# Two padding tensors that move matmul operands to 64 bytes past a multiple of 128

## The chip, the cores and the metric

The kernel runs on one core of one Trainium2 chip, as one launch. The metric is the device time in microseconds of one execution; the numbers given are medians of several runs, and one execution is taken by the hardware profiler.

## The reference, cut to what matters

Two small networks follow each other on 256 tokens of width 1024, each with two layers, all in float32. A layer of the first network is a feed-forward block, a mixer with three branches (a linear recurrence, a latent attention with 8 heads, a convolution branch) whose outputs are gated and merged, and a second feed-forward block. A layer of the second network is a mixer (16 attention heads of four kinds) and one feed-forward block with a short convolution.

```python
def swiglu(x, w1, w2):
    gu = x @ w1
    g, u = gu[..., :D_FF], gu[..., D_FF:]
    return (jax.nn.silu(g) * u) @ w2

for l in range(DEPTH):
    x = x + 0.5 * swiglu(rms_norm(x, ffn1_norm[l]), ffn1_w1[l], ffn1_w2[l])
    x = x + hybrid_mixer(rms_norm(x, mix_norm[l]), ...)
    x = x + 0.5 * swiglu(rms_norm(x, ffn2_norm[l]), ffn2_w1[l], ffn2_w2[l])
```

D_FF is 2816, so a feed-forward block holds 1024 x 5632 and 2816 x 1024 weights. All weights are read from HBM once; nothing of them is reused.

## The kernel before, in words

Activations lie transposed, features on the 128 partitions and the 256 tokens along the free dimension, in tiles of 128 features: h is 8 such tiles, the hidden layer 22. The weights are cut into blocks of 128x128, and up to 16 blocks make a unit of at most 1 MB. A unit comes by one DMA into one of two raw buffers, in a fixed order (ALL_UNITS).

To reach float32 accuracy at the rate of the faster type fp32r, a number is split into a high part (rounded to fp32r) and the low remainder. ScalarE copies raw to w_hi (split_hi, line 597), VectorE subtracts to w_lo (split_lo, line 636); there are four slots of each. Activations are split the same way: h_hi and h_lo, hid_hi and hid_lo (the hidden layer), m_hi and m_lo (the merged branches of mixer 1), o2_hi and o2_lo (the heads' outputs of mixer 2), win_hi and win_lo (windows of keys and values in mixer 2). A product of a weight block and a tile is three matmuls that add up in PSUM (product, lines 657 to 659): high with high, high weight with low activation, low weight with high activation. The weight block is the stationary operand, loaded by an LDWEIGHTS of its own for each matmul, and the activation moves, 256 columns of 4 bytes. first_products (669 to 678) and by_tiles (692 to 694) issue the same matmuls in another order. In tokens_product (710 to 712) the roles are swapped: the weights move and h or win is stationary. Other products (whole_product, 704, attention scores, transposes, norm sums) are matmuls in plain float32; the weights of these come to w_whole, w_lat, scr or sq.

A feed-forward block is an up stage of 22 units of 16 blocks (48 matmuls each on h) and a down stage of 8 output tiles with two units of 11 blocks (66 matmuls each tile on hid). Between them VectorE scales, multiplies and splits, ScalarE applies silu. In mixer 1, UNIT_ORDER1 gives the order: 11 units of two tiles on h, the recurrence, the latent projections (uq, uk), the attention, then the branch products A, B and C with their gates (24 tiles on h) and the output product on m. In mixer 2, STEPS2 gives it: nine units of features on h, the values, and 24 heads, one after the other, among which other units stand.

Every tensor of SBUF is placed by the order of its sbuf(...) line, one after the other, sizes rounded up to 32 bytes. Tensors of one `with ExitStack()` block share their place with those of the next. The first, raw, begins at byte 16,512 of each partition, which is 129 x 128. So the program before has these addresses modulo 128: raw, w_hi, w_lo, x, h_hi, h_lo, const, vec, scr, sq, acc, std and rinv at 0; rinv is 258 numbers long, so trig1, cos2, sin2 and all that begins behind them (hid_hi, hid_lo, m_hi, m_lo, feat, win, win_hi, win_lo, o2_hi, o2_lo, const2) at 32. Farther up, conv, gelu, xa and w_whole are at 0, and lat, w_lat, o1 and v2a at 64.

LAT_BLOCKS says how many of the 12 blocks of unit ("uq", 2) lie in w_lat; the others lie in sq. Line 601 copies the first, line 603 the rest.

Of the kernel before, what the change touches and what calls it, by code (L numbers as in the profile page):

```python
# [16 lines left out]
F32 = mybir.dt.float32  # L17
# [6 lines left out]
T = 256  # L24
P = 128
# [8 lines left out]
SPLIT_SLOTS = 4  # L34
AHEAD = 3
FFN_AHEAD = 4
EPS = 1e-6
MASKED = -1e30
TWO_PI = 2 * np.pi
# [250 lines left out]
def build(nc, io):  # L290
    with ExitStack() as ctx:
        def sbuf(name, shape, dt=F32, stack=ctx):
            return stack.enter_context(nc.sbuf_tensor(name, shape, dt))
# [2 lines left out]
        raw = sbuf("raw", [P, RAW_SLOTS, 16 * P])  # L296
        w_hi = sbuf("w_hi", [P, SPLIT_SLOTS, 16 * P], F32R)
        w_lo = sbuf("w_lo", [P, SPLIT_SLOTS, 16 * P], F32R)
        x = sbuf("x", [P, KT, T])
        h_hi = sbuf("h_hi", [P, KT, T], F32R)  # L300
        h_lo = sbuf("h_lo", [P, KT, T], F32R)
# [3 lines left out]
        sq = sbuf("sq", [P, 2, T])  # L305
# [3 lines left out]
        trig1 = sbuf("trig1", [P, T])  # L309
        cos2 = sbuf("cos2", [P, T])  # L310
        sin2 = sbuf("sin2", [P, T])
        ones = const[:, CONST["ones"]:CONST["ones"] + P]
        ident = const[:, CONST["ident"]:CONST["ident"] + P]
        causal = const[:, CONST["causal"]:CONST["causal"] + 384]
# [10 lines left out]
        with ExitStack() as phase:  # L325
            with ExitStack() as early:
                q1 = sbuf("q1", [P, QKV_HEADS, T], F32, early)
                k1 = sbuf("k1", [P, QKV_HEADS, T], F32, early)
            m_hi = sbuf("m_hi", [P, KT, T], F32R, phase)
            m_lo = sbuf("m_lo", [P, KT, T], F32R, phase)  # L330
            v1 = sbuf("v1", [P, 2, QKV_HEADS * VD], F32, phase)
            glu = sbuf("glu", [P, 4, T + CONV_TAPS - 1], F32, phase)
            conv = sbuf("conv", [P, 4, T], F32, phase)
            derived = sbuf("derived", [P, 64], F32, phase)
            probs1 = sbuf("probs1", [P, 2, 384], F32, phase)
            probs_t1 = sbuf("probs_t1", [P, 2, 384], F32, phase)
            row1 = sbuf("row1", [P, 16], F32, phase)
            with ExitStack() as early:
                lat = sbuf("lat", [P, 5, T], F32, early)
                w_lat = sbuf("w_lat", [P, 22 * P], F32, early)  # L340
            o1 = sbuf("o1", [P, 4, T], F32, phase)
            sbuf("rest", [P, 3, 4, T], F32, phase)
            pad_r = sbuf("pad_r", [P, 4, T + LRU_TAPS - 1], F32, phase)
            gelu = sbuf("gelu", [P, 4, T], F32, phase)
            xa = sbuf("xa", [P, 4, T], F32, phase)
            a_t = sbuf("a_t", [P, 4, T], F32, phase)
            i_g = sbuf("i_g", [P, 4, T], F32, phase)
            w_whole = sbuf("w_whole", [P, SPLIT_SLOTS * 4 * P], F32, phase)
            with ExitStack() as early:
                r_g = sbuf("r_g", [P, 4, T], F32, early)  # L350
            gate = sbuf("gate", [P, 2, T], F32, phase)
            y_b = sbuf("y_b", [P, 2, T], F32, phase)
# [205 lines left out]

        LAT_BLOCKS = 10

        def unit_kind(s):

            return UNIT_ORDER1[s % len(UNITS1) - MIX1_AT]
# [1 line left out]
        def whole_part(s, block, blocks):  # L567

            unit = unit_kind(s)
            if unit == ("uk", 0):  # L570
                return scr[:].rearrange("p k t -> p (k t)")[:, block * P:(block + blocks) * P]
            if unit == ("uq", 2) and block >= LAT_BLOCKS:
                return sq[:, 0, (block - LAT_BLOCKS) * P:(block - LAT_BLOCKS + blocks) * P]
            if unit[0] == "uq":
                at = block + (12 if unit[1] else 0)
                return w_lat[:, at * P:(at + blocks) * P]
            at = (4 * (s % SPLIT_SLOTS) if PARTED[s] else 0) + block
            return w_whole[:, at * P:(at + blocks) * P]
# [8 lines left out]
        def split_hi(act, s, more=0, half=0):  # L587
# [10 lines left out]
            if parted < n:  # L598
                count = (n - parted) // P
                cut = LAT_BLOCKS if unit_kind(s) == ("uq", 2) else count  # L600
                last = act.activation(whole_part(s, 0, cut), raw[:, s % RAW_SLOTS, parted:parted + cut * P], ACT.Copy)
# [290 lines left out]
        def ffn_act(act, l, w, at, then, split):  # L892
# [9 lines left out]
            with act.Fori(0, 4) as it:  # L902
                for u in range(4):
                    gated(u, it * 4, u % 2, lambda: split_hi(act, at + u + FFN_AHEAD, it * 4, it * 2))
            split.next = at + 16 + FFN_AHEAD
            for j in range(16, FT):
                gated(j, 0, j % 2, lambda: split.until(at + j + FFN_AHEAD))
            if l == 0 and w == 0:
                act.wait_ge(*turned(0, 1))
                act.activation(trig1[:], trig1[:], ACT.Sin).then_inc(trig_ready.sem, 1)  # L910
            if l == 0 and w == 1:
                act.wait_ge(*turned2(0, 2))
                act.activation(cos2[:], cos2[:], ACT.Sin)
                act.activation(sin2[:], sin2[:], ACT.Sin).then_inc(trig2_ready.sem, 1)
            base = at + FT + FFN_AHEAD
            l2, n2_ = then
# [21 lines left out]
        def ffn_dve(dve, l, w, at, n, then, split):  # L938
# [20 lines left out]
            for j in range(2):  # L959
                gated(j, 0, j % 2, lambda: split.until(at + j + FFN_AHEAD), j > 0)  # L960
            with dve.Fori(0, 4) as it:
                for u in range(2, 6):
                    gated(u, it * 4, u % 2, lambda: split_lo(dve, at + u + FFN_AHEAD, it * 4))
            split.next = at + 18 + FFN_AHEAD
# [1121 lines left out]
        block = ctx.enter_context(nc.Block())  # L2086
# [385 lines left out]
```

## Time and profile before

| | us |
|---|---|
| median of 3 runs | 2106.05 |
| lowest and highest run | 2103.4, 2112.19 |
| the profiled execution | 2109.53 |
| its span, first to last instruction | 2107.7 |
| PE busy in the span | 2003.4 |
| DVE busy | 1406.4 |
| ACT busy | 1160.2 |
| mean granted clock of TensorE | 0.977 |

The page gives the busy time of each engine (PE is the matmul side of TensorE, PEld its weight loads, DVE VectorE, ACT ScalarE, POOL GpSimd). Start times are measured; the ends of matmuls are modelled, so a matmul's duration (some 280 ns) is longer than the distance from its start to the next. The rows on which the prediction rests stand two sections below.

### The profile page before, as it was taken

How to read it: one execution, taken by the hardware profiler on the slowest of the kernel's cores; microseconds unless marked ns; L12 is line 12 of the kernel's file. 1: busy time of each engine (PE TensorE's matmuls, PEld its weight loads, DVE VectorE, ACT ScalarE, POOL GpSimd, SP SyncE). 2: the span in 40 equal slices, each digit the busy share in tenths (PEclk: the TensorE clock that was granted, in tenths of full speed). 3: DMA queues.
4: the chain of work that ended last, by engine and by line, in shares of the span. 5: the costliest groups of instructions: out<-in, count | busy, mean ns of one | idle time of the engine just before them, and what ended most of it. 6: DMA issues, size and time to landing. Idle time of an engine off the chain costs nothing.

```text
span 2107.7 us, 39543 instructions
## 1 busy us (share of the span) xinstructions
PE 2003.4 (95%) x15240; PEld 1901.6 (90%) x15240; DVE 1406.4 (67%) x2072; ACT 1160.2 (55%) x1847; POOL 142.3 (7%) x153
## 2 busy tenths in 40 slices
PE   7999989989999999989989999998999999898998
PEld 7999969989999999978989999976899998678997
DVE  5765887666655665788656656775588568738973
ACT  5444666554445444576455445575666457656753
POOL 1062100010000000100000001000100010002000
PEclk9999999999999999999999999998999999999999
DMA  5545433445545545443445545441245544304543
GB/s 213 206 169 185 150 125 125 151 170 184 185 156 194 198 158 186 167 151 105 153 163 181 193 149 183 162 160 41 81 164 197 173 154 152 137 3 156 202 163 116
DMA packets 53533, 329.80 MB, mean 156 GB/s; under 512 B 5936, under 2 KB 6704, under 8 KB 27952
## 3 DMA queue, kind: packets, MB, share of 16 engines
q1 hardware_dynamic: 53424, 328.34, 44.5%
q8 instruction: 69, 1.13, 0.2%
q14 instruction: 40, 0.33, 0.0%
HBM read 327.27 MB, written 1.05 MB: 156 GB/s over the span
## 4 chain that ended last, share of the span: by engine, by line
PE 61%; DVE 13%; issue 8%; ACT 6%; DVEq 5%; DMA 4%; POOLq 3%; POOL 1%; ACTq 0%; SPq 0%
PE bank L657 16%; PE bank L658 16%; PE bank L659 16%; DVE w_lo L636 5%; DMA raw<-in_w 4%; PE bank L704 3%; ACT w_hi L597 2%; DVE conv L1362 1%; PE bank L669 1%; PE bank L1651 1%; PE bank L671 1%; PE bank L1635 1%; DVEq L1356 1%; PE bank L1652 1%; PE bank L1653 1%
## 5 line engine op out<-in xcount | busy, mean ns | idle before, releaser
L636 DVE TENSOR_TENSOR w_lo<-raw,w_hi 128x2048 fp32r<-128x2048 f32 (+3 forms) x348 | 673.6, 1939 | 343.5 <-ACT w_hi L597 316.2
L657 PE MATMUL bank<-h_hi,w_hi 128*128 128x256 f32 x2704 | 779.2, 288 | 8.4 <-DVE conv L2024 3.4
L658 PE MATMUL bank<-h_lo,w_hi 128*128 128x256 f32 x2704 | 768.0, 284 | 0.0
L659 PE MATMUL bank<-h_hi,w_lo 128*128 128x256 f32 x2704 | 767.6, 284 | 0.0
L597 ACT ACTIVATE w_hi<-raw 128x2048 fp32r<-128x2048 f32 (+2 forms) x346 | 560.3, 1623 | 142.2 <-DMA raw<-in_w 118.6
L657 PEld LDWEIGHTS bank<-h_hi,w_hi 128*128 128x128 f32 x2704 | 522.0, 193 | 14.9 <-issue 8.5
L658 PEld LDWEIGHTS bank<-h_lo,w_hi 128*128 128x128 f32 x2704 | 522.1, 193 | 1.2
L659 PEld LDWEIGHTS bank<-h_hi,w_lo 128*128 128x128 f32 x2704 | 521.8, 193 | 0.0
L657 PE MATMUL bank<-hid_hi,w_hi 128*128 128x256 f32 x1056 | 295.4, 280 | 0.0
L658 PE MATMUL bank<-hid_lo,w_hi 128*128 128x256 f32 x1056 | 295.4, 280 | 0.0
L659 PE MATMUL bank<-hid_hi,w_lo 128*128 128x256 f32 x1056 | 295.3, 280 | 0.0
L657 PEld LDWEIGHTS bank<-hid_hi,w_hi 128*128 128x128 f32 x1056 | 198.5, 188 | 0.0
L658 PEld LDWEIGHTS bank<-hid_lo,w_hi 128*128 128x128 f32 x1056 | 198.5, 188 | 0.0
L659 PEld LDWEIGHTS bank<-hid_hi,w_lo 128*128 128x128 f32 x1056 | 198.5, 188 | 0.0
L897 ACT ACTIVATE scaled<-scaled 128x256 f32<-128x256 f32 x88 | 36.8, 418 | 258.3 <-DVE scaled L944 258.3
L796 POOL TENSOR_TENSOR acc<-sq 128x256 f32<-128x256 f32 x13 | 12.2, 940 | 1577.9 <-ACT sq L789 1577.7
L1362 DVE SCALAR_TENSOR_TENSOR conv<-glu,vec,conv 128x256 f32<-128x256 f32 x240 | 106.0, 481 | 10.7 <-issue 0.9
L789 ACT ACTIVATE sq<-x 128x256 f32<-128x256 f32 (+1 forms) x88 | 35.9, 410 | 123.1 <-DVE x L974 92.6
L944 DVE TENSOR_TENSOR scaled<-bank,rinv 128x512 f32<-128x512 f32 x88 | 60.6, 689 | 50.6 <-PE bank L659 37.1
L669 PE MATMUL bank<-h_hi,w_hi 128*128 128x256 f32 x224 | 64.8, 321 | 18.2 <-DVEq L1913 6.6
L800 POOL TENSOR_TENSOR acc<-acc,sq 128x256 f32<-128x256 f32 x65 | 60.3, 928 | 227.2 <-ACT sq L789 224.4
L669 PEld LDWEIGHTS bank<-h_hi,w_hi 128*128 128x128 f32 x224 | 50.8, 227 | 20.6 <-DVEq L1913 7.4
(339 smaller groups left out, 2960.5 us busy)
## 6 DMA issues: line engine op xcount, KB each, us to landing
raw<-in_w SPq DMA_DIRECT2D x198, 1024.0 KB, 4.8
raw<-in_w SPq DMA_DIRECT2D x96, 704.0 KB, 4.1
raw<-in_w SPq DMA_DIRECT2D x52, 768.0 KB, 4.2
raw<-in_w SPq DMA_DIRECT2D x8, 512.0 KB, 3.5
raw<-in_w SPq DMA_DIRECT2D x4, 576.0 KB, 3.7
x<-in_x SPq DMA_DIRECT2D x1, 1024.0 KB, 5.0
out<-x SPq DMA_DIRECT2D x4, 256.0 KB, 2.4
const<-in_const SPq DMA_DIRECT2D x1, 548.0 KB, 5.7
```

The lines of the kernel that those rows point to most:

```text
L597: last = act.activation(w_hi[:, s % SPLIT_SLOTS, 0:parted], raw[:, s % RAW_SLOTS, 0:parted], ACT.Copy)
L636: dve.tensor_tensor(w_lo[:, s % SPLIT_SLOTS, 0:n], raw[:, s % RAW_SLOTS, 0:n], w_hi[:, s % SPLIT_SLOTS, 0:n].bitcast(F32), ALU.subtract).t ...
L657: pe.matmul(out, hi, x_hi, start=start, stop=False, skip_group_check=skip)
L658: pe.matmul(out, hi, x_lo, start=False, stop=False, skip_group_check=skip)
L659: return pe.matmul(out, lo, x_hi, start=False, stop=stop, skip_group_check=skip)
L669: pe.matmul(out, w_hi[:, s % SPLIT_SLOTS, at], h_hi[:, k], start=k == 0 and half == 0, stop=False, skip_group_check=half == 1)
L704: return pe.matmul(out, whole_part(s, block, 1), y, start=start, stop=stop)
L789: act.activation(sq[:, parity], src, ACT.Square).then_inc(nm.sq_ready.sem, 1)
L800: pool.tensor_tensor(acc[:], acc[:], sq[:, t % 2], ALU.add).then_inc(nm.sq_summed.sem, 2 if t == KT - 2 else 1)
L897: act.activation(scaled[:, parity, 0:T], scaled[:, parity, 0:T], ACT.Silu).then_inc(silu_ready.sem, 1)
L944: dve.tensor_tensor(halves(scaled[:, parity]), halves(bank[:, :]), by_r(2), ALU.mult).then_inc(work.freed["v"].sem, 1)
L1362: last = dve.scalar_tensor_tensor(conv[:, t], glu[:, t, j:j + T], w, conv[:, t], ALU.mult, ALU.add)
```

## The change

Two tensors are added that nothing reads or writes, offset_h of 16 numbers (64 bytes) behind w_lo, and offset_hid of 24 numbers (96 bytes) behind sin2. They take room, so w_lat shrinks by one block: LAT_BLOCKS goes from 10 to 9 and moves to the head of the file, and the tensor `rest` (which only keeps room for lat and w_lat behind o1) is written by its new size. The third block of unit ("uq", 2) that now lies in sq runs into sq's second half, so sq is addressed flat.

The addresses modulo 128 that follow: raw, w_hi and w_lo stay at 0; x, h_hi, h_lo, const, vec, scr, sq, acc, std and rinv go from 0 to 64; trig1, cos2 and sin2 from 32 to 96; hid, m, feat, win, o2 and const2 from 32 to 64; conv, gelu, xa and w_whole from 0 to 32; lat, w_lat, o1 and v2a from 64 to 96.

```diff
@@ -34,6 +34,7 @@
 FFN_AHEAD = 4
+LAT_BLOCKS = 9
 EPS = 1e-6
@@ -296,6 +297,7 @@
         w_lo = sbuf("w_lo", [P, SPLIT_SLOTS, 16 * P], F32R)
+        sbuf("offset_h", [P, 16])
         x = sbuf("x", [P, KT, T])
@@ -309,6 +311,7 @@
         sin2 = sbuf("sin2", [P, T])
+        sbuf("offset_hid", [P, 24])
         ones = const[:, CONST["ones"]:CONST["ones"] + P]
@@ -337,9 +340,9 @@
                 lat = sbuf("lat", [P, 5, T], F32, early)
-                w_lat = sbuf("w_lat", [P, 22 * P], F32, early)
+                w_lat = sbuf("w_lat", [P, (12 + LAT_BLOCKS) * P], F32, early)
             o1 = sbuf("o1", [P, 4, T], F32, phase)
-            sbuf("rest", [P, 3, 4, T], F32, phase)
+            sbuf("rest", [P, T + (12 + LAT_BLOCKS) * P], F32, phase)
@@ -558,8 +561,6 @@
-        LAT_BLOCKS = 10
-
@@ -570,7 +571,7 @@
             if unit == ("uq", 2) and block >= LAT_BLOCKS:
-                return sq[:, 0, (block - LAT_BLOCKS) * P:(block - LAT_BLOCKS + blocks) * P]
+                return sq[:].rearrange("p a t -> p (a t)")[:, (block - LAT_BLOCKS) * P:(block - LAT_BLOCKS + blocks) * P]
```

## Rows read from the trace of the kernel before

**Rows 1.** The page, part 1: busy us, share of the span, instructions.

```profile
PE 2003.4 (95%) x15240; PEld 1901.6 (90%) x15240; DVE 1406.4 (67%) x2072; ACT 1160.2 (55%) x1847; POOL 142.3 (7%) x153
```

**Rows 2.** Windows by stage: busy us (count) per engine, PEclk, DMA, GB/s.

```profile
663.00:790.00 127.00, 127.00 (x1058) 126.89 (x1057) 80.70 (x86) 58.94 (x70) 0.00 (x0) 1.00 0.51 178
790.00:852.00 62.00, 62.00 (x530) 62.00 (x530) 33.60 (x33) 27.50 (x31) 5.90 (x6) 1.00 0.56 192
852.00:1116.00 264.00, 243.30 (x1700) 226.63 (x1699) 194.41 (x346) 158.25 (x270) 12.82 (x14) 0.98 0.42 147
1508.00:1641.00 133.00, 130.04 (x1058) 128.33 (x1058) 115.19 (x173) 89.36 (x132) 11.83 (x14) 0.99 0.48 168
...
1703.00:1902.00 199.00, 181.67 (x1166) 150.50 (x1165) 132.38 (x249) 123.94 (x275) 5.38 (x6) 0.95 0.31 107
```

**Rows 3.** Timeline, PE, up stage: start us, duration us, line, operation.

```profile
60.03 0.28 PE L658 MATMUL bank<-h_lo,w_hi 128*128 128x256 f32 x1
...
61.11 0.28 PE L658 MATMUL bank<-h_lo,w_hi 128*128 128x256 f32 x1
```

**Rows 4.** Timeline, PE in a down stage.

```profile
151.00 0.28 PE L659 MATMUL bank<-hid_hi,w_lo 128*128 128x256 f32 x1
151.12 0.28 PE L657 MATMUL bank<-hid_hi,w_hi 128*128 128x256 f32 x1
151.23 0.28 PE L658 MATMUL bank<-hid_lo,w_hi 128*128 128x256 f32 x1
...
151.94 0.28 PE L658 MATMUL bank<-hid_lo,w_hi 128*128 128x256 f32 x1
```

**Rows 5.** Timeline, PE in mixer 1 (m) and mixer 2 (weights moving).

```profile
464.13 0.28 PE L658 MATMUL bank<-m_lo,w_hi 128*128 128x256 f32 x1
...
465.19 0.28 PE L658 MATMUL bank<-m_lo,w_hi 128*128 128x256 f32 x1
...
1352.81 0.39 PE L711 MATMUL bank<-w_hi,h_lo 128*128 128x512 f32 x1
1353.04 0.40 PE L712 MATMUL bank<-w_lo,h_hi 128*128 128x512 f32 x1
```

**Rows 6.** Groups by form: count, busy us, mean ns of one, idle before.

```profile
L658 PEld LDWEIGHTS bank<-h_lo,w_hi 128*128 128x128 f32 x2704 | 522.1, 193 | 1.2
...
L658 PE MATMUL bank<-hid_lo,w_hi 128*128 128x256 f32 x1056 | 295.4, 280 | 0.0
...
L658 PEld LDWEIGHTS bank<-hid_lo,w_hi 128*128 128x128 f32 x1056 | 198.5, 188 | 0.0
...
L704 PE MATMUL bank<-o,w_whole 128*128 128x256 f32 x128 | 30.3, 379 | 0.0
...
L704 PE MATMUL bank<-conv,w_whole 128*128 128x256 f32 x128 | 29.6, 379 | 0.0
...
L711 PE MATMUL bank<-w_hi,win_lo 128*128 128x256 f32 x64 | 17.9, 280 | 0.0
```

**Rows 7.** Groups by form, DVE and ACT.

```profile
L636 DVE TENSOR_TENSOR w_lo<-raw,w_hi 128x2048 fp32r<-128x2048 f32 x198 | 452.4, 2289 | 177.7 <-ACT w_hi L597 177.1
L597 ACT ACTIVATE w_hi<-raw 128x2048 fp32r<-128x2048 f32 x196 | 372.8, 1906 | 83.1 <-DMA raw<-in_w 80.1 <-PE bank L659 1.9 <-PE bank L694 0.5
...
L636 DVE TENSOR_TENSOR w_lo<-raw,w_hi 128x1408 fp32r<-128x1408 f32 x92 | 150.1, 1632 | 136.8 <-ACT w_hi L597 136.7
L597 ACT ACTIVATE w_hi<-raw 128x1408 fp32r<-128x1408 f32 x92 | 126.4, 1375 | 49.9 <-DMA raw<-in_w 29.4 <-PE bank L659 20.3
...
L949 DVE TENSOR_TENSOR hid<-scaled 128x256 f32<-128x256 f32 x88 | 37.6, 428 | 14.9 <-ACT scaled L897 12.6
...
L1497 DVE TENSOR_TENSOR scr<-scr,sq 128x256 f32<-128x256 f32 x32 | 13.6, 426 | 2.7
```

**Rows 8.** DMA issues by line: count, KB each, median us to landing.

```profile
raw<-in_w SPq DMA_DIRECT2D x198, 1024.0 KB, 4.8
raw<-in_w SPq DMA_DIRECT2D x96, 704.0 KB, 4.1
```

## The prediction

> **What bounds the kernel now.** I read the page's busy shares first: TensorE (PE) is busy 95% of the span, VectorE (DVE) 67%, ScalarE (ACT) 55%, and the DMA engines about half [rows 1]. A busy share is an average, so I cut the span into stages and took a window of each [rows 2]. The up stage of a feed-forward block is 127.0 us of unbroken PE work, its down stage 62.0 us, both at a granted clock of 1.00 (the 2.4 GHz level). Four feed-forward blocks of this kind belong to the first network and two to the second, whose up stage takes 133.0 us with DVE busy 115.2. The mixers take 264 and 199 us, with PE busy 243.3 and 181.7 and the clock at 0.98 and 0.95. So about 1150 of 2108 us are stages in which PE never waits, and their length is a number of matmuls times the distance from one start to the next.
>
> That distance is what the change can touch. Ends of matmuls are modelled, so I take starts. In the up stage nine steps take 60.03 to 61.11 us, 120.0 ns each [rows 3]. In the down stage eight steps take 151.00 to 151.94 us, 117.5 ns, and the whole stage gives 62.0 us / 528 matmuls = 117.4 ns [rows 2, 4]. Both move 256 columns against a 128x128 weight block, at the same granted clock. 256 columns at 2.4 GHz are 106.7 ns, so the up stage pays 13.3 ns more and the down stage 10.7 ns. What differs is the operand's address: h_hi and h_lo lie at 0 modulo 128 bytes like the weights, hid_hi and hid_lo at 32. Other pairs sort the same way. m_hi and m_lo (at 32) take 464.13 to 465.19 us for nine steps, 117.8 ns, by the same lines and in the same banks that h uses [rows 5]. With the weights as the moving side, 512 columns against h (both at 0) come 0.23 us apart where 213.3 ns would be the columns alone, and 256 columns against win (32) have a mean duration of 280 ns, the same as hid [rows 5, 6]. The weight loads agree: 193 ns beside h, 188 ns beside hid [rows 6]. I conclude that TensorE's two read streams, moving operand and next weight block, disturb each other, and that their addresses relative to each other set by how much.
>
> The Trainium skill ("TensorE: Matmul & The Clock Gate", on what each phase is for) speaks against this: the moving operand and the weight load have independent read ports, and loading the next block doesn't take bandwidth from the running matmul. It gives N / 2.4 + 2.5 ns for a warm matmul, an estimate of 109.2 ns for 256 columns. By that rule the address can't matter and the change is worth nothing; the trace disagrees with both halves of it (120.0 and 117.4 ns).
>
> **The change, part by part.** (1) h_hi and h_lo go from 0 to 64 modulo 128, the weights w_hi and w_lo stay at 0. (2) hid, m, o2 and win go from 32 to 64. No row shows an fp32r pair 64 apart, so the cost is bounded. Upper end: as if the 64 were 0, 120.0 ns. Lower end: the columns alone, 106.7 ns. Between them I take the straight continuation of the two measured points, 120.0 at 0 and 117.4 at 32, which is 114.8 at 64. Single steps of 0.11 us already stand beside steps of 0.12 in the down stage (151.12 to 151.23) [rows 4], so this value is near what the trace shows to be reachable. h then gains 5.2 ns, the others 2.6 ns.
>
> The counts come from the code: an up stage has 22 x 48 = 1056 matmuls on h, a down stage 8 x 66 = 528 on hid; mixer 1 has 11 x 48 + 24 x 24 = 1104 on h and 192 on m; mixer 2 has 408 + 96 = 504 on h and 288 on o2 and win. The windows' counts agree for the stages (1058, 530) [rows 2].
> - First network, up: 4 x 1056 x 5.2 = 22.0 us, all of it, as PE never waits there. Down: 4 x 528 x 2.6 = 5.5 us.
> - Second network, down: 2 x 528 x 2.6 = 2.7 us. Up: 2 x 1056 x 5.2 = 11.0 us, but DVE has 115.2 / 22 = 5.24 us a unit against PE's 48 x 120 = 5.76, and PE is already idle for 3 of the 133 us [rows 2]. With 5.51 us a unit PE would still be the longer one; I count 70%, 7.7 us.
> - Mixer 1: 2 x (1104 x 5.2 + 192 x 2.6) = 12.5 us. PE is busy 92% of the stage, yet the gaps wait on DVE and ACT chains which don't get shorter; I count 70%, 8.7 us (bounds 0 and 12.5).
> - Mixer 2: 2 x (504 x 5.2 + 288 x 2.6) = 6.7 us. Head by head PE, ACT and DVE hand over to each other; I count half, 3.4 us (bounds 0 and 6.7).
>
> The sum is 50.0 us. What may come late next: a raw buffer is held for the landing, the high half and the low half, 4.8 + 1.91 + 2.29 = 9.0 us in the up stage and 4.1 + 1.38 + 1.63 = 7.1 us in the down stage [rows 7, 8]; with two buffers that is 4.5 and 3.6 us a unit, below PE's 5.51 and 33 x 114.8 = 3.79 us. So the weight stream still hides, the down stage with little to spare.
>
> (3) The plain fp32 matmuls (L704) also change addresses: conv with w_whole (both at 0) and o with w_whole (64 and 0) both take 379 ns [rows 6]. They are not sensitive; I count nothing, bounds +-1 ns x 500 = +-0.5 us. (4) DVE and ACT tiles move too. A DVE multiply of 256 columns at address 32 (hid, L949) takes 428 ns, a sum at 0 (scr, L1497) 426 [rows 7]. Nothing, and PE covers them where it is the bound. (5) The DMA targets raw stay where they are; x, const and vec move by 64 bytes. x is 1 MB, as a unit of raw is, which lands in 4.8 us [rows 8]; a tenth longer would be 0.5 us at the start, which no work hides, and vec lands between layers under other work. I take 0. (6) The tenth block of unit uq 2 moves from w_lat to sq: the same two ACT copies, of 9 and 3 blocks where they were 10 and 2, no new instruction and no new wait; the next writers of sq come with the mixer's B products. Nothing, and if ACT's split cost more, the mixer's slack covers it.
>
> The profiled execution took 2109.5 us with a span of 2107.7; the median of the three runs is 2106.05. The sum is made on the profiled one and is 2.4% of it, so I set it against the median: 2106 - 50 = **2056 us**.
>
> **The rivals.**
> - A, the forecast: the disturbance falls on with distance up to 64, 114.8 ns, 2056 us. For it: both measured levels, the same on hid, m and win. Chance 0.43; its own range is 2035 to 2075 (113 to 116.5 ns, and the mixers' share from a third to all).
> - B, 64 does what 32 does: 117.4 ns for all, hid gains nothing. 11.0 + 3.8 + 4.0 + 1.3 = 20.1 us, 2086 us. Chance 0.15. For it: the first step away may be all there is.
> - C, the pattern repeats every 64 bytes. Then 64 is as bad as 0: h stays at 120.0 and hid, m, o2 and win, until now the lucky ones at 32, rise to it. 3168 x 2.6 = 8.2 us in the down stages and 1.5 in the mixers, 2116 us, +0.46%. It decides as soon as 64 costs more than about 119 ns: h's gain of 9552 x 1 ns is then eaten by the others' loss. For it: rows at 32 to either side of the weights (hid, and weights moving past win) look alike, which a period of 64 explains as well as one of 128. Were 64 even worse than 0, by 1 ns, it would be some 10 us more. Chance 0.20, of which half lies over +0.5%.
> - D, at 64 the streams hardly meet: about 110 ns. h gains 10.0 ns and the others 7.4: 42.2 + 15.6 + 14.8 + 7.8 + 17.4 + 7.2 = 105 us, 2001 us; the down stage's unit would be 3.63 us, just above the 3.56 of the raw buffers. Chance 0.13.
> - E, the address isn't the cause and nothing moves: 2106 us. The up and down stages also differ in how banks alternate; m in h's banks speaks against it. The skill's rule of independent ports, named above, would give this time. Chance 0.09.
>
> **How the numbers follow.** The measurement tells 0.5% from no change, 2095.5 to 2116.6 us. Faster: A, B and D, 0.71. Within: E and half of C, 0.19. Slower: the other half of C, 0.10. The range must hold 8 in 10: it reaches up to C (2117) and down past A's own end into D's upper part, 2008 us; it leaves out most of D and C's worse half.
>
> **What would show it.** In the up stage, the distance of starts on L657 to L659: 0.115 us is A, 0.117 B, 0.120 C or E, 0.110 D; the down stage tells C (0.120) from E (0.117). The up stages should take 121.5 us in place of 127, the down stages 60.6 in place of 62; LDWEIGHTS beside h below 188 ns. The second network's up stage should gain less than the first's, with waits of PE for conv (L2024) grown. Matmuls on w_whole should stay at 379 ns. Wrong would be: PE's distances shrink and the stages don't (the weight stream or DVE took over), or DVE's and ACT's own durations moved.

## The result, and the profile after

The changed kernel took 2092.51 us (median; 2091.18 to 2097.16) against 2106.09 us before: a ratio of 0.9937, 95% interval 0.9921 to 0.9954. So it is 13.6 us faster, inside the range, where 50 us were forecast. The profiled execution took 2097.16 us with a span of 2095.4, 12.3 us less than the one before. Line numbers after are one higher: the products are L658 to L660.

The page's first part answers [rows 1], and nothing but PE has moved:

```profile
PE 1987.6 (95%) x15240; PEld 1883.0 (90%) x15240; DVE 1406.4 (67%) x2072; ACT 1160.9 (55%) x1847; POOL 141.3 (7%) x153
```

The first thing to read is the distance of starts. Timeline of PE in the first up stage after (start, duration, engine, line), for [rows 3]:

```profile
100.03 0.28 PE L660 MATMUL bank<-h_hi,w_lo 128*128 128x256 f32 x1
100.15 0.28 PE L658 MATMUL bank<-h_hi,w_hi 128*128 128x256 f32 x1
100.27 0.28 PE L659 MATMUL bank<-h_lo,w_hi 128*128 128x256 f32 x1
...
100.97 0.28 PE L659 MATMUL bank<-h_lo,w_hi 128*128 128x256 f32 x1
101.09 0.28 PE L660 MATMUL bank<-h_hi,w_lo 128*128 128x256 f32 x1
```

Nine steps take 1.06 us, 117.8 ns each, where it was 120.0. That is not the 114.8 ns of the forecast; it is what the down stage had before, or a little more. The windows of the same stages as [rows 2], each cut at the new times (length, then PE, PEld, DVE, ACT, POOL busy, the granted clock, DMA share, GB/s):

```profile
659.00:784.00 125.00, 125.00 (x1061) 124.90 (x1060) 80.51 (x86) 59.02 (x70) 0.00 (x0) 1.00 0.51 181
784.00:846.00 62.00, 62.00 (x529) 62.00 (x528) 33.58 (x33) 27.59 (x31) 5.91 (x6) 1.00 0.56 192
846.00:1108.00 262.00, 242.20 (x1700) 223.71 (x1700) 194.65 (x347) 158.76 (x270) 12.60 (x14) 0.97 0.42 148
1497.00:1630.00 133.00, 129.30 (x1057) 127.54 (x1057) 115.55 (x174) 89.89 (x132) 11.84 (x14) 0.98 0.48 168
1692.00:1891.00 199.00, 181.32 (x1171) 149.70 (x1170) 132.39 (x249) 124.12 (x275) 5.37 (x6) 0.95 0.31 108
```

The undisturbed up stage fell from 127 to 125 us (exactly, 127.7 to 125.3); the down stage stayed at 62, and its starts are 117.8 ns apart, where they were 117.4: hid gained nothing and lost 0.4 ns. The mixer is 2 us shorter than its 264, the second network's up stage (133) and mixer (199) stayed within the microsecond that a window can tell. Cut exactly, from the start of a stage's first matmul to that of the next stage's, and summed over all stages of a kind (us):

| stages | before | after | difference | forecast |
|---|---|---|---|---|
| up, first network (4) | 514.67 | 506.98 | -7.7 | -22.0 |
| down (6) | 374.07 | 375.63 | +1.6 | -8.2 |
| up, second network (2) | 268.33 | 266.67 | -1.7 | -7.7 |
| mixer 1 (2) | 528.45 | 525.82 | -2.6 | -8.7 |
| mixer 2 (2) | 399.16 | 397.18 | -2.0 | -3.4 |
| sum | 2084.69 | 2072.28 | -12.4 | -50.0 |

The groups agree with the timeline, for [rows 6]: a modelled h matmul is 4 ns shorter than before (284 for 288 on the line shown), the weight load beside it 189 instead of 193 ns, hid within 1 ns.

```profile
L658 PE MATMUL bank<-h_hi,w_hi 128*128 128x256 f32 x2704 | 769.1, 284 | 12.0 <-DVE w_lo L637 5.0
...
L659 PEld LDWEIGHTS bank<-h_lo,w_hi 128*128 128x128 f32 x2704 | 510.6, 189 | 1.1
...
L658 PE MATMUL bank<-hid_hi,w_hi 128*128 128x256 f32 x1056 | 295.0, 279 | 0.0
```

So the change does act by the distance of starts, and the question is why 64 bytes give 117.8 ns. In what follows "distance" is the time between two starts and "difference" the address of the moving operand less that of the weight block.

### The profile page after: what moved, and what is told of

It is laid out like the page before. It is cut to its first block, busy times and chain, and to the rows that moved or that the text cites. A ratio compares the mean times of both kernels' runs of the same rounds, so it can differ in the third digit from the quotient of the medians.

```text
span 2095.4 us, 39543 instructions
## 1 busy us (share of the span) xinstructions
PE 1987.6 (95%) x15240; PEld 1883.0 (90%) x15240; DVE 1406.4 (67%) x2072; ACT 1160.9 (55%) x1847; POOL 141.3 (7%) x153
## 4 chain that ended last, share of the span: by engine, by line
PE 72%; DVE 12%; ACT 6%; DVEq 4%; issue 3%; DMA 3%; POOL 0%; POOLq 0%; ACTq 0%; SPq 0%
PE bank L658 19%; PE bank L660 19%; PE bank L659 19%; DVE w_lo L637 4%; PE bank L705 3%; DMA raw<-in_w 2%; ACT w_hi L598 2%; DVE conv L1363 1%; PE bank L1636 1%; PE bank L670 1%; PE bank L672 1%; PE bank L1652 1%; DVEq L1357 1%; PE bank L679 1%; DVE x L1923 1%
## 5 line engine op out<-in xcount | busy, mean ns | idle before, releaser
L658 PE MATMUL bank<-h_hi,w_hi 128*128 128x256 f32 x2704 | 769.1, 284 | 12.0 <-DVE w_lo L637 5.0
L660 PE MATMUL bank<-h_hi,w_lo 128*128 128x256 f32 x2704 | 757.8, 280 | 0.0
L659 PE MATMUL bank<-h_lo,w_hi 128*128 128x256 f32 x2704 | 757.6, 280 | 0.0
L658 PEld LDWEIGHTS bank<-h_hi,w_hi 128*128 128x128 f32 x2704 | 510.1, 189 | 19.0 <-DVE w_lo L637 9.2
L659 PEld LDWEIGHTS bank<-h_lo,w_hi 128*128 128x128 f32 x2704 | 510.6, 189 | 1.1
L660 PEld LDWEIGHTS bank<-h_hi,w_lo 128*128 128x128 f32 x2704 | 510.3, 189 | 0.0
L660 PE MATMUL bank<-hid_hi,w_lo 128*128 128x256 f32 x1056 | 295.1, 279 | 0.0
L658 PE MATMUL bank<-hid_hi,w_hi 128*128 128x256 f32 x1056 | 295.0, 279 | 0.0
L660 PEld LDWEIGHTS bank<-hid_hi,w_lo 128*128 128x128 f32 x1056 | 198.2, 188 | 0.0
L658 PEld LDWEIGHTS bank<-hid_hi,w_hi 128*128 128x128 f32 x1056 | 197.9, 187 | 0.0
L797 POOL TENSOR_TENSOR acc<-sq 128x256 f32<-128x256 f32 x13 | 12.2, 942 | 1564.0 <-ACT sq L790 1563.8
L790 ACT ACTIVATE sq<-x 128x256 f32<-128x256 f32 (+1 forms) x88 | 36.0, 411 | 125.0 <-DVE x L975 93.1
L670 PE MATMUL bank<-h_hi,w_hi 128*128 128x256 f32 x224 | 63.4, 316 | 17.8 <-DVEq L1914 6.6
L670 PEld LDWEIGHTS bank<-h_hi,w_hi 128*128 128x128 f32 x224 | 49.6, 221 | 20.2 <-DVEq L1914 7.4
```

Source lines behind the costliest of these rows:

```text
L658: pe.matmul(out, hi, x_hi, start=start, stop=False, skip_group_check=skip)
L659: pe.matmul(out, hi, x_lo, start=False, stop=False, skip_group_check=skip)
L660: return pe.matmul(out, lo, x_hi, start=False, stop=stop, skip_group_check=skip)
L670: pe.matmul(out, w_hi[:, s % SPLIT_SLOTS, at], h_hi[:, k], start=k == 0 and half == 0, stop=False, skip_group_check=half == 1)
L790: act.activation(sq[:, parity], src, ACT.Square).then_inc(nm.sq_ready.sem, 1)
```

## The experiments

The kernels named m leave out the networks and run TensorE alone, mostly 64 to 96 matmuls for each pair of addresses (48 or 24 where said), in a fixed order and in one execution each. A mean there leaves out the first four starts of a series and is then (last start - first start) / (count - 1), from the trace's starts in ns. The kernels named e are the whole kernel. "Before" was run again beside each group of them: 2107.13 us (e5, e1, e2), 2107.24 (e4, e7) and 2105.63 (e8, e9, e0).

**m1_map: the distance at each difference.** Edit: a kernel of only

```python
for n in range(96):   # once for each pair of offsets at_w, at_m (in numbers of 4 bytes)
    pe.matmul(banks[(n // 8) % 8][0:128, 0:256], wts[:, at_w + P * (n % 16):][:, 0:128], mov[:, at_m + 256 * (n % 16):][:, 0:256], ...)   # cut: start and stop of each 8
```

> Leaves out the whole computation: x is copied to the output, and TensorE alone runs series of 96 (some 48) fp32r matmuls of 256 columns, each with its own 128x128 weight block, one series for each start address of the moving operand (0, 16, 32, ... 128, 160, 192 bytes past a multiple of 128, and 4, 8, 12, 24, 40, 56, 72) with the weights at 0; then pairs with the weights moved (32, 64, 96 with moving at 0; 32 with 32, 64 with 64, 32 with 96). Theory 1, a step: only the exact coincidence modulo 128 is slow. 120.0 ns from start to start at 0 and 128, between 117 and 118 ns at every other multiple of 16, 192 like 64; 32 with 32 and 64 with 64 are 120 again since only the difference counts. Theory 2, a period of 128 with a slope: the forecast's 114.8 ns at 64 comes back here and the 117.8 ns of the changed kernel came from something else in it (VectorE or ScalarE reading beside). Theory 3, the moving operand's own address counts and not the difference: 32 with 32 gives 117.4, and weights at 32 with moving at 0 gives 120.

Measured, with the weights at 0 and the moving operand at so many bytes:

| bytes | 0 | 16 | 32 | 48 | 64 | 80 | 96 | 112 | 128 | 160 | 192 |
|---|---|---|---|---|---|---|---|---|---|---|---|
| ns | 120.00 | 118.65 | 116.66 | 118.34 | 117.77 | 119.95 | 119.98 | 113.33 | 118.65 | 117.33 | 113.38 |

Single lines and operands of m1_map (duration least, median, most; first and last start), the moving operand at 0, 32, 64 and 112 bytes:

```profile
L62 PE MATMUL bank<-mov,wts x96: 283/283/284, 29.2 to 40.6; 128*128 128x256 f32 x96
...
L68 PE MATMUL bank<-mov,wts x96: 277/279/282, 52.1 to 63.2; 128*128 128x256 f32 x96
...
L74 PE MATMUL bank<-mov,wts x96: 279/279/284, 74.6 to 85.8; 128*128 128x256 f32 x96
...
L83 PE MATMUL bank<-mov,wts x96: 275/275/276, 109.0 to 119.8; 128*128 128x256 f32 x96
```

95 steps take 11.4, 11.1, 11.2 and 10.8 us. The address alone, with no other engine at work, makes the kernel's own 120.0 and 117.8 ns. The curve is no slope: 64 is worse than 32, 80 and 96 are nearly as bad as 0, and 112 is better than all. Nor does it repeat after 128 bytes: 128 is not 0, and 192 is not 64. Moving both operands together changes nothing (both at 32: 119.93; both at 64: 120.00), and weights at 64 with the moving operand at 0 (a difference of 192) give 113.34. One pair does not fit: weights at 96 and moving at 0, a difference of 160, gave 120.00 and not 117.33. The seven series between the 16-byte steps (48 matmuls each) are no better: 123.37 at 4 bytes, the slowest of all, 119.72 at 8, 117.74 at 12, 120.00 at 24, 119.91 at 40, 119.67 at 56 and 120.30 at 72. So all three theories fail: 128 isn't 120.0 (1), 64 isn't 114.8 (2), and both at 32 isn't 117.4 (3).

This also put a name to an error in my reading. The weights w_hi and w_lo lie at 128 modulo 256. Before, h's difference was 0, but that of hid and m, which I had called 32, is 160; after, all have 64. Nor do all tensors of that group stand alike: win is 4480 bytes long, 128 past a multiple of 256, so win_hi, o2_hi and o2_lo went from 32 to 192 bytes past the weights, and win_lo from 160 to 64 (for win, where the weights move, the difference has the other sign). In the traces the unbroken series of matmuls on win took a mean of 118.0 ns a step before and 114.1 after, those on o2 117.1 and 115.4. These terms gained, while hid lost.

**m2_width: what part of the matmul carries the excess.** Edit: m1_map's loop with other widths, at differences of 0, 32 and 64.

> Leaves out the whole computation as the map of addresses does. TensorE runs series at moving addresses 0, 32 and 64 with weight blocks of 128, 96, 64 and 32 columns (the moving side 256 columns), then 512 and 128 moving columns, then plain float32. Theory 1, the next weight block's reading disturbs the running matmul: at 0 the excess over 106.7 ns (13.3 ns with 128 weight columns) falls about in proportion, to 8 ns with 64 columns and 5 ns with 32, and the differences between the addresses shrink with it; with 512 moving columns the excess stays 13.3 ns. Theory 2, the excess belongs to the moving operand's own start (its first read is at an unlucky place): 13.3 ns at 0 whatever the number of weight columns, and a steady 11 ns at 32 and 64. Plain float32: 216 ns at all three addresses by both.

| ns at 0 / 32 / 64 | |
|---|---|
| 256 columns, 128 weight columns | 120.00 / 117.75 / 117.77 |
| 256 columns, 96 weight columns | 116.01 / 116.68 / 113.33 |
| 256 columns, 64 weight columns | 113.33 / 119.05 / 113.33 |
| 256 columns, 32 weight columns | 117.78 / 120.00 / 116.67 |
| 512 columns, 128 weight columns | 226.86 / 233.32 / 228.95 |
| 128 columns, 128 weight columns | 111.70 / 111.66 / 111.64 |
| plain float32, 256 columns | 215.84 / 215.84 / 215.84 |

Neither theory holds: the excess changes with the number of weight columns at a fixed address, but doesn't fall steadily with it, nor is it the same for all. At 512 columns the order is reversed, 32 being the worst. Two of the rows matter for the kernel. Single lines of m2_width, 128 moving columns at 0 and plain float32 at 0 and 32:

```profile
L107 PE MATMUL bank<-mov,wts x96: 222/274/277, 207.8 to 218.3; 128*128 128x128 f32 x96
...
L116 PE MATMUL bank<-mf,wf x96: 379/379/431, 239.9 to 260.5; 128*128 128x256 f32 x96
...
L119 PE MATMUL bank<-mf,wf x96: 379/379/379, 260.7 to 281.2; 128*128 128x256 f32 x96
```

With half the columns a step still takes 111.7 ns, at each of the three differences tried. Half the columns are 53.3 ns at 2.4 GHz, so I take it that the 128x128 weight block, which each matmul brings along, sets this time. That is argued and not shown: no run had 128 moving columns with fewer weight columns. If it is so, no address brings the kernel's matmuls below about 111.7 ns, and rival D's 110 was out of reach. And plain float32 is the same 215.84 ns (and 379 ns of duration) at all three: the w_whole matmuls can't feel the change, as the prediction had it from [rows 6].

**m3_order: is it the difference modulo 256, and does the order matter?** Edit: 64 matmuls at each difference from 0 to 480 in steps of 32, rising, then many of them again in a mixed order.

> Leaves out the whole computation, as the map of addresses does. 64 matmuls for each moving address from 0 to 480 in steps of 32, in rising order, then the same (and 112) in a shuffled order. Theory 1, a fixed function of the difference modulo 256: both orders give the same, 120.0 ns at 0 and 256, 117.8 at 64 and 320, 113.3 at 192 and 448. Theory 2, the pair falls into one of a few beats (113.3, 116.7, 117.8, 120.0 ns), and which one depends also on where it comes from: some addresses give two values, 128 and 96 first of all, which didn't look like a function of the difference modulo 128 in the map.

Rising: 0 120.00, 32 117.75, 64 117.76, 96 119.86, 128 118.66, 160 117.34, 192 113.34, 224 118.31, and from 256 to 480 the same eight. So in steps of 32 the pattern repeats after 256 bytes. In the mixed order 64, 96, 224, 0 and 256 kept their value within 0.12 ns, but 192 came out at 117.76 when entered from 128, 32 at 116.66 (117.75 before), 160 at 118.78 (117.34 before), and 384, which is 128 again, at 120.02 (118.66 before). Some differences have more than one steady distance (a beat, from here on), and what went before seems to pick one. 64 showed only one here; it did not stay so.

**e5_h192_hid192: the change with 192 in place of 64.** Edit, from the changed kernel (192 bytes of padding instead of 64, so that all later operands move with it):

```diff
-        sbuf("offset_h", [P, 16])
+        sbuf("offset_h", [P, 48])
```

> The changed kernel with 192 bytes in front of x in place of 64: h, hid and m now start 192 bytes (modulo 256) beyond the weights. If the map of addresses holds inside the kernel, starts are 113.3 ns apart: the up stages save 6336 x 6.7 = 42 us and the down stages 3168 x 4.1 = 13 us against before, less what the second network's VectorE and the mixers keep; 2055 to 2065 us. Theory 2, the beat depends on the history and on what the other engines read: 117 to 118 ns here too, about 2092 us, as the kernel changed.

Measured: 2070.44 us (2064.54 to 2080.93), ratio 0.9844 (0.9824 to 0.9864), some 5 us above the expected 2055 to 2065. In its trace all up and down stages run at 113.33 ns but the last layer's, which run at 117.78: its up stage from 1868.5 us on, with one unit of 48 matmuls at 113.3 in between (1904.9 us), and its whole down stage. Two stages of the same code in one execution with two beats: m3_order's finding in the kernel, and a possible part of why its runs are spread over 16 us. The gain is not all there either, because the first down stage took 71.0 us, longer than before (63.6). Waits of e5_h192_hid192 from 110 to 215 us (engine, line and tile, what was waited for: us in total, times, longest):

```profile
POOL scr L2237 <- DMA scr<-in_pos: 96.7, 1, 96.7
DVE w_lo L637 <- ACT w_hi L598: 45.7, 22, 14.4
...
ACT sq L790 <- POOL acc L797: 14.3, 1, 14.3
...
PE bank L658 <- DVE w_lo L637: 5.4, 1, 5.4
```

Read from the bottom: PE waits 5.4 us for a low half, whose DVE waits up to 14.4 us for the high half on ACT, which itself stands 14.3 us in front of a square (L790) because GpSimd's sum (L797) is late. GpSimd's sum starts at 169.0 us, and at 168.6 us in the kernel before: it did not get later, the others came earlier. GpSimd is late because its first task, reducing the rotary angles, waited 96.7 us for the positions (scr from in_pos), whose DMAs are issued behind all weight units of the first up stage. With a slower PE the same chain was there and all but hidden: in the changed kernel ACT's wait is 7.6 us and PE does not wait for a low half in this stretch. The wait cost more than its length: right behind it the granted clock stood at 0.52 over 172.5 to 179.5 us, and 26 matmuls came 213 ns apart (the 1.2 GHz level), 2.6 us more.

**e1_h64_hid32: hid back by 32 bytes.** Edit, from the changed kernel:

```diff
-        sbuf("offset_hid", [P, 24])
+        sbuf("offset_hid", [P, 16])
```

> The changed kernel with hid, m, o2 and win back at 32 and h at 64. If the two addresses act each by itself: up stages as in the changed kernel (117.8 ns), down stages as before (117.4 ns), 1.3 us faster than the changed kernel, about 2091 us. If 64 for both mattered together: slower than the changed kernel by more than 3 us.

Measured: 2090.93 us (2090.68 to 2103.32), ratio 0.9937 (0.9919 to 0.9956). h at 117.78; hid at 116.67 ns in five down stages (61.6 us each) and at 120.0 in the first. It is the changed kernel's time within the interval, as forecast, but from another pair of beats than the forecast had; 32 has at least three of them (116.67, 117.75, 120.0).

**e2_hid64: only hid's part of the change.** Edit, from before (32 bytes more in front of hid; h stays at difference 0):

```diff
+        sbuf("offset_hid", [P, 8])
```

> The kernel before with hid, m, o2 and win at 64 and h left at 0. Each by itself: up stages 120.0 ns, down stages 117.8 ns, 1 to 2 us slower than before, 2107 to 2108 us. If the gain of the change came from hid or from the tiles behind it: near 2092 us.

Measured: 2096.53 us (2091.34 to 2099.76), ratio 0.9951 (0.9939 to 0.9964). This was a miss, and the most useful one. Timeline and a window of e2_hid64 in a down stage:

```profile
799.67 0.28 PE L659 MATMUL bank<-hid_lo,w_hi 128*128 128x256 f32 x1
799.78 0.28 PE L660 MATMUL bank<-hid_hi,w_lo 128*128 128x256 f32 x1
799.90 0.28 PE L658 MATMUL bank<-hid_hi,w_hi 128*128 128x256 f32 x1
...
800.24 0.28 PE L658 MATMUL bank<-hid_hi,w_hi 128*128 128x256 f32 x1
```

```profile
785.00:845.00 60.00, 60.00 (x531) 60.00 (x530) 33.40 (x34) 27.83 (x31) 5.89 (x6) 1.00 0.59 197
```

Five steps from 799.67 to 800.24 are 114 ns, and 528 matmuls take 59.9 instead of 62.0 us: 113.33 ns in all six down stages. Here hid lies at 64 modulo 128 like in the changed kernel, but its difference to the weights is 192 modulo 256, and there 113.33 is what m1_map gives. The undisturbed up stage is as before, 127.7 us, so the gain of 2.1 us a down stage is the move of hid alone.

**m4_entry: which lead-in picks the beat.** Edit: m1_map's loop, 72 matmuls at one difference, each after 24 at 0, 64, 128 or 32.

> Leaves out the whole computation. TensorE alone: each of the moving addresses 192, 112, 144, 176, 208 and 240 (weights at 0) for 72 matmuls, four times, entered from 24 matmuls at 0, 64, 128 or 32. Theory 1, a function of the difference modulo 256 alone: 192 gives 113.3 ns whatever came before. Theory 2, two beats are stable at 192 and the lead-in picks one: 113.3 ns after 0 and 32, 117.8 ns after 64 (whose own beat is 117.8) and after 128. 112 gave 113.3 twice; if it has one beat only, it does so after all four.

Single lines of m4_entry, difference 192 entered from 0 and from 128, and one of the six lead-ins at 64:

```profile
L65 PE MATMUL bank<-mov,wts x72: 276/276/286, 32.1 to 40.1; 128*128 128x256 f32 x72
...
L77 PE MATMUL bank<-mov,wts x72: 281/281/283, 54.1 to 62.5; 128*128 128x256 f32 x72
...
L140 PE MATMUL bank<-mov,wts x24: 276/276/280, 174.7 to 177.3; 128*128 128x256 f32 x24
```

71 steps take 8.0 and 8.4 us; exactly, 192 came out at 113.33 after 0, 113.34 after 64, 113.33 after 32 and **117.76** after 128. The expectation that 64 leads to the slow beat was wrong, and so the entry explains m3_order but not yet e5_h192_hid192, where h at 192 was slow in one layer after plain matmuls and waits. Difference 112 settled at 113.3 after each of the four (means 113.33 to 113.88, since after three of them the first dozen steps were longer). The others: 144 at 118.6, 176 at 119.3, 208 at 119.2, 240 at 117.2. The lead-ins show one thing more. Five of the six at 64 ran at 117.8, but the fourth, behind a series at 176, ran its 24 matmuls at 113.32 (L140, 23 steps in 2.6 us): 64 has two beats as well. So has 128: four of its lead-ins lie at 118.5 to 118.9, two at 119.9 to 120.0.

**e4_block_only: the weight block moved, no padding.** Edit: the changed kernel without its two padding tensors; what stays is `LAT_BLOCKS = 9` with the sizes that go with it.

> The changed kernel without the two padding tensors: the moved latent block and the new size of rest alone, all matmul operands where they were. If the addresses of h and hid are the whole cause: as before, 2104 to 2109 us, starts 120.0 and 117.4 ns apart. If the moved block had a part in the 13 us: faster than before by more than 3 us.

Measured: 2107.98 us (2102.66 to 2111.95), ratio 1.0001 (0.999 to 1.0013), the beats as before. The block's move costs nothing, and all of the change's effect is in the padding.

**e7_h64_hid192: h as in the change, hid at 192.** Edit, from the changed kernel:

```diff
-        sbuf("offset_hid", [P, 24])
+        sbuf("offset_hid", [P, 56])
```

> The changed kernel with 128 bytes more in front of hid: h stays 64 bytes beyond the weights modulo 256 (117.8 ns there), hid, m go from 64 to 192. Theory 1, the difference modulo 256 alone: hid at 113.3 ns as in the kernel with hid alone moved, 3168 x 4.4 = 14 us faster than the changed kernel, about 2079 us. Theory 2, the beat is inherited from the stage before: the down stage enters from 117.8 ns and stays there, about 2092 us.

Measured: 2087.09 us (2083.09 to 2097.97), ratio 0.9925 (0.9901 to 0.9949). That is neither the 2079 nor the 2092 us of the two theories, because each came out in part: four down stages at 113.3, two (from 139.3 and 1618.2 us) at 117.78, and all six entered from h at 117.8. The trace of e7_h64_hid192 in the first and the third down stage, by the same lines and tiles:

```profile
149.81 0.28 PE L660 MATMUL bank<-hid_hi,w_lo 128*128 128x256 f32 x1
149.92 0.28 PE L658 MATMUL bank<-hid_hi,w_hi 128*128 128x256 f32 x1
...
150.87 0.28 PE L660 MATMUL bank<-hid_hi,w_lo 128*128 128x256 f32 x1
...
799.73 0.28 PE L660 MATMUL bank<-hid_hi,w_lo 128*128 128x256 f32 x1
799.84 0.28 PE L658 MATMUL bank<-hid_hi,w_hi 128*128 128x256 f32 x1
...
800.75 0.28 PE L660 MATMUL bank<-hid_hi,w_lo 128*128 128x256 f32 x1
```

Nine steps are 1.06 us in the one and 1.02 us in the other: 117.8 and 113.3 ns, of the same addresses in one execution. A beat, once taken, is held for a whole stage of 528 matmuls as long as nothing interrupts it. The distance of the lead-in alone doesn't pick it.

**e8_h112_hid112: the difference with one good beat.** Each pair of high and low halves becomes one tensor with a 16-byte lead, so that h, hid and m lie at 112. From the changed kernel, cut to h (hid_hi, hid_lo, m_hi and m_lo alike; offset_hid and a spacer adjusted to fit):

```diff
+        def tiles_at(both, at, tiles):
+            return both[:, at:at + tiles * T].rearrange("p (k t) -> p k t", t=T)
-        sbuf("offset_h", [P, 16])
-        h_hi = sbuf("h_hi", [P, KT, T], F32R)
-        h_lo = sbuf("h_lo", [P, KT, T], F32R)
+        sbuf("offset_h", [P, 24])
+        h_both = sbuf("h_both", [P, 4 + 2 * KT * T], F32R)
+        h_hi, h_lo = (tiles_at(h_both, 4 + n * KT * T, KT) for n in range(2))
```

> The changed kernel with h, hid and m 112 bytes beyond the weights modulo 256 (h_hi and h_lo lie in one tensor, so do the other pairs, so that 16-byte steps are possible). 112 gave 113.3 ns after every lead-in. Theory 2 (each difference has its stable beats; 112 has one): every up and down stage at 113.3 ns in this and every other execution; up stages 6336 x 6.7 and down stages 3168 x 4.1 ns less than before, about 2060 us, and a narrower spread than the 2064 to 2081 us of the kernel at 192. Rival, only a multiple of 64 can hold the fast beat beside the running VectorE and ScalarE: 117 to 120 ns, 2090 us or more.

Measured: 2061.07 us (2056.19 to 2068.03), ratio 0.9795 (0.9774 to 0.9815). Every up and down stage settles at 113.33 ns; where a wait interrupts one, as in the second network's up stages, the first dozen steps behind it are longer (116 to 119 ns), and then it is 113.3 again. The undisturbed up stage takes 120.8 us, the undisturbed down stages 59.8. I had expected runs closer together than those of e5_h192_hid192, and they still lie 12 us apart: with five runs of each, 192's two beats don't explain the spread. The rival, which held that only a multiple of 64 keeps the fast beat, is refuted. The first down stage is again long, 68.7 us, PE waiting 3.4 us behind the same chain (ACT 12.6 us in front of its square). Of the 8.9 us over 59.8, the wait is 3.4, the 17 matmuls behind it at the 1.2 GHz level 1.7, and a second pause, before mixer 1, 3.4.

**e9_h112_pos: the positions earlier.** Edit, from e8_h112_hid112: SyncE issues the two position DMAs right behind the first two weight units instead of behind the first up stage's last.

```diff
+                    load_loop(sp, packed(io["w1"], UNITS1, at, l, FT), g, FT, 2 if g == 0 else 0, positions if g == 0 else None)
-                        if l == 0:
-                            sp.dma_start(pos_i, io["pos1"].to_broadcast([P, T])).then_inc(pos_in.sem, 16)
-                            sp.dma_start(pos2_i, io["pos2"].to_broadcast([P, T])).then_inc(pos_in.sem, 16)
```

> As the kernel at 112, and the two position loads leave right behind the first two weight units in place of 110 us later, so that GpSimd's angle reduction is over before the first down stage. In the kernel at 192 ScalarE waited 14.3 us there for GpSimd's first sum of squares and TensorE 5.4 us for the low halves behind it. If that is a wait the faster beat laid bare: 5 to 10 us faster than the kernel at 112. If it was chance: the same time.

Measured: 2051.06 us (2045.5 to 2058.22), ratio 0.9724 (0.9705 to 0.9744). Timeline of PE in the up stage of e9_h112_pos, and windows of its first up and down stages:

```profile
100.04 0.28 PE L661 MATMUL bank<-h_both,w_hi 128*128 128x256 f32 x1
100.15 0.28 PE L662 MATMUL bank<-h_both,w_hi 128*128 128x256 f32 x1
100.26 0.28 PE L663 MATMUL bank<-h_both,w_lo 128*128 128x256 f32 x1
...
101.06 0.28 PE L661 MATMUL bank<-h_both,w_hi 128*128 128x256 f32 x1
```

```profile
30.00:152.00 122.00, 122.00 (x1079) 122.00 (x1078) 83.50 (x92) 59.16 (x73) 39.44 (x34) 1.00 0.56 195
152.00:212.00 60.00, 59.38 (x516) 58.93 (x516) 35.02 (x35) 33.19 (x39) 12.22 (x14) 1.00 0.59 200
```

Nine steps of 113.3 ns, PE busy without a gap in a window that spans the turn from the up to the down stage; the first down stage takes 59.8 us where e8_h112_hid112 took 68.7. GpSimd's work now stands in the up stage (39.4 us), where nothing waits for it. It is 10 us faster than e8_h112_hid112, the upper end of what was expected, though the two profiles don't show that difference: e9's is the slowest of its five runs (2058.22), e8's the fastest of its five (2056.19), and in them the 8.9 us of the first down stage are set off against mixers 2 that take 5.3 and 3.6 us longer. It is 55 us faster than before and 45 us faster than the changed kernel run beside it: more than the forecast hoped for, from another address and an earlier DMA.

**e0_changed_again: does 64 ever take another beat?** No edit: the changed kernel once more, beside e8_h112_hid112 and e9_h112_pos.

> The changed kernel once more, on the chip of the other two. If 64 has one beat: all stages at 117.8 ns again, 2091 to 2097 us. If 117.8 was one of two: some stage at 113.3 ns.

Measured: 2096.18 us (2090.58 to 2099.1), ratio 0.9949 (0.9929 to 0.9969), all long stretches at 117.78 again. But 117.78 is one of two. Among the h matmuls of this trace stand eight short series at 113.3 ns, and twelve in the changed kernel's (336 of some 8900 steps), none longer than a unit of 48 matmuls. Timeline of e0_changed_again, a unit of mixer 2:

```profile
1760.62 0.28 PE L660 MATMUL bank<-h_hi,w_lo 128*128 128x256 f32 x1
...
1765.72 0.28 PE L660 MATMUL bank<-h_hi,w_lo 128*128 128x256 f32 x1
```

45 steps in 5.10 us are 113.3 ns, at a difference of 64. In the changed kernel such a unit (1523.7 to 1528.8 us) stands in the second network's up stage, between others at 117.8. So the 2092 us rest on the slower of the two beats of 64, and what holds it there in nearly all stages is not known.

## Why the prediction was right in direction and wrong in size

**The cause was right.** The prediction concluded from [rows 3 to 6] that the moving operand's address relative to the weights sets the distance of starts. m1_map shows it with TensorE alone, e4_block_only shows that nothing else in the change acts, and rival E falls. That the two read streams disturb each other, as the prediction put it, is not shown: a form of it, with an excess in proportion to the weight columns, was refuted by m2_width. And the rows were sorted modulo 128, which put hid and m (160 past the weights) and win_hi (32 past them) under one level, 117.4 ns. That these lie within 1 ns of each other was chance. The Trainium skill ("TensorE: Matmul & The Clock Gate", on what each phase is for) states that loading the next weights takes nothing from the running matmul's reads; by it no difference would matter, and 113.3 to 120.0 ns by the address alone speak against it.

**The step that failed is the size at 64:** "the straight continuation of the two measured points, 120.0 at 0 and 117.4 at 32, which is 114.8 at 64". What stood in its place is 117.8 ns at 64. The step was wrong in two ways. The point called 32 was 160: the differences had been taken modulo 128, and the pattern repeats after 256 (m3_order, and e2_hid64 in the kernel, where 64 modulo 128 gave 113.33 and not 117.78). And there is no line to continue: the distance takes one of a few values in no order (120.0 at 0, 118.7 at 16, 117.8 at 64, 120.0 at 80 and 96, 113.3 at 112). Two points can't show either. The lower bound was loose too: 106.7 ns from the columns alone is below the 111.7 ns that matmuls of half as many columns take (m2_width).

**Point by point, in the prediction's order:**
- h: 117.8 instead of 114.8, a gain of 2.2 ns for 5.2. 4 x 1056 x 2.2 = 9.3 us; the first network's up stages gave 7.7. The rest is the granted clock: in the four stages 67 matmuls came some 213 ns apart (the 1.2 GHz level) where before it was 53, and 14 x 95 ns = 1.3 us. Their number goes by the execution: with h at 64 it was 54 in e1_h64_hid32 and 80 in e0_changed_again.
- hid: a loss of 0.4 ns for a gain of 2.6. 3168 x 0.4 = 1.3 us, measured 1.6 us. The sign of this term was wrong.
- The shares: with 2.2 ns the second network's up stages could give 4.6 us and gave 1.7 (37%, I had 70%); 72 of their matmuls stood at the 1.2 GHz level for 54 before, which is 1.7 us of the shortfall. Mixer 1 could give 4.9 less 0.2 for m, and gave 2.6 (55%; I had 70%). Mixer 2 could give 2.2 on h, and some 1.4 more on win and o2 by the means above, and gave 2.0 (I had half). Of the last the profiles tell little, since a mixer's length differs between executions (the first of mixer 2 took 195.0 us in e8_h112_hid112 and 200.3 in e9_h112_pos, by the same code). With the measured distances and my own shares the sum is 9.3 - 1.3 + 3.2 + 3.3 + 1.1 = 15.6 us, against 12.4 measured; so of the 37.6 us that were missing the distance cost 34.4 and shares and clock the other 3.
- The rivals: B (117.4 ns, 2086 us) was nearest, right for h and too kind to hid, which it left at no change; I had given it a chance of 0.15. C's idea, that hid might rise, is where hid's loss lies, but its period of 64 is refuted (0 at 120.0 and 64 at 117.8 in m1_map, m2_width and m3_order). D's 110 ns was seen in no run; 113.3 was the least at 256 columns.
- Nothing from w_whole, DVE, ACT and the weight block: right. w_whole's durations don't depend on the address (m2_width), DVE is at 1406 us, and e4_block_only measured the block at 1.0001.
- "So the weight stream still hides, the down stage with little to spare": right down to 113.3 ns, where the down stages take 59.8 us with no gap. What came late at 113.3 ns was something that the prediction had not looked at: GpSimd's angle reduction in the first down stage, held up by position DMAs queued behind 22 weight units (e5_h192_hid192, e8_h112_hid112), and it is removed by e9_h112_pos.

**What stays open:** why a difference gives the distance that it gives, and what picks a beat where there are two. m2_width refuted both of my theories of the first; m4_entry and e7_h64_hid192 refuted those of the second that go by the lead-in's distance alone.

## What to carry to other kernels

Where TensorE is the bound and every matmul brings its own weight block, measure the distance of starts in the trace and sweep the moving operand's address against the weights' modulo 256 in steps of 16 bytes, in a short kernel of matmuls alone; never continue a line through two points. Enter each candidate from several others, look at the lead-ins too, and take one that settles at the same distance each time (112 here, in every series and stage), as another may come with two (192, and even 64). Then look at what is late once TensorE is faster: here a wait behind GpSimd, in a stage that had been at most 1.6 us longer than its like (63.6 against 62.0), came to cost it 9 us (68.7 against 59.8), partly through the granted clock that fell behind it.

## What the runs showed of the hardware

- The distance of fp32r matmuls of 256 columns, each with its own 128x128 weights, is 113.3 to 120.0 ns at a granted clock of 1.00, by the address difference modulo 256 in steps of 16 bytes (m1_map, m3_order, m4_entry); a difference of 4 bytes gave 123.4. At 2.4 GHz 113.33 is 272 periods, 16 over the columns, and 120.00 is 288, 32 over; nothing lower than 113.3 was seen.
- Many differences have two or more steady distances: 192 (113.33 and 117.78) and 32 (116.67, 117.75 and 120.0), each held for tens to hundreds of matmuls, 160 (117.3, 118.8, and 120.0 with the weights moved), 128 (118.7 and 120.0), and 64 (117.78 nearly always, 113.3 for 24 matmuls in m4_entry and for single units in the kernel). 112 settled at 113.3 everywhere.
- Behind a wait of TensorE of 3.4 us (e8_h112_hid112) and one of 5.4 us (e5_h192_hid192) the granted clock fell to one half, and 17 and 26 matmuls came 213 ns apart.
- 128 columns take 111.7 ns at each of the three differences tried (0, 32, 64), and plain float32 of 256 columns takes 215.84 ns at each (m2_width).
- Fewer weight columns are not steadily faster: at a difference of 0, 120.00 ns with 128 of them, 116.01 with 96, 113.33 with 64 and 117.78 with 32 (m2_width, one series each; at 32, where 120.00 came with 32 weight columns, 128 of them give three values by themselves).
